# Latent attention on one core: the order of three engines inside a group of two heads

## The chip, the cores and the metric

One core of one Trainium2 chip runs the whole program. The metric is the device time of one execution in microseconds; lower is better. The time of the kernel before is the median of 3 runs.

The engines: PE is TensorE (matmuls; PEld is its weight loads, which run beside them), DVE is VectorE, ACT is ScalarE, POOL is GpSimd, SP issues DMAs. Each engine works through its own list in the order in which it is written, and waits at semaphores for the others.

## What is computed

The reference is two blocks of a network, with float32 throughout. The change touches one operation in the first block, the latent attention (8 heads of 64 + 32 features, 256 context tokens and 1024 latent tokens):

```python
def block_attention(q, k, v, scale):            # per block of 128 queries
    s = jnp.einsum('bhqd,bhkd->bhqk', qi, k) * scale
    p = jax.nn.softmax(s, axis=-1)
    return jnp.einsum('bhqk,bhkd->bhqd', p, v)

# latent queries see context and latent keys, context queries the context keys
a_lat = block_attention(qa_l, concat([ka_c, ka_l]), concat([va_c, va_l]), scale)
a_ctx = block_attention(qa_c, ka_c, va_c, scale)
```

The queries are `rmsnorm(cq) @ w_uq`, whose last 32 features of each head are rotated by position. Everything else in the program (projections, mLSTM, gated linear attention, neighbourhood attention, a second block with an MLP) stands before or behind this loop and stays as it is.

## The kernel before

The attention is a loop over 40 groups in `mla_block`. A group g is a pair of heads and a tile of 128 queries: `groups[g] = (j, t)`. Its two heads are u = 2g (head 0) and u = 2g+1 (head 1). The first 8 groups are of context queries and have 2 key tiles of 128 keys each (short groups); the other 32 are of latent queries and have 10 (long groups).

The scores are made with the keys in the partitions: one key tile gives a 128 x 128 piece of scores, key by query. Head 0 has its scores in three PSUM banks (`S[0]`), head 1 in three others (`S[1]`). A float32 matmul of the source is two matmul instructions in the trace, each with its weight load: a key tile of scores is 2 loads, 10 tiles are 20.

For one head the steps are, in the order in which they depend on each other:

- `score` (TensorE, L1034): the key tiles' scores. A head's first tile waits for the rotated queries (`q_ev`) and until the head before the last in the same banks has been subtracted (`lowered`).
- `tops` (VectorE, L1332): the maximum over the key tiles, for each query and each of the 128 key rows.
- `turn_top` (TensorE, L1043): turns that 128 x 128 piece, so that queries are in the partitions. It waits for `tops`.
- `highest` (VectorE, L1336): one maximum for each query.
- `spread_max` (TensorE, L1047): turns the maxima into a row that stands in all partitions. It waits for `highest`.
- `copy_max` (ScalarE, L1226): copies that row from PSUM.
- `lower` (VectorE, L1342): subtracts the row from all scores. It waits for `copy_max`.
- `soft` (ScalarE, L1237): the exponential.
- `key_sums` (GpSimd, L889 to L894): adds up the key tiles for the softmax's denominator.

Per group come `weigh` (TensorE, L1055: 40 narrow matmuls over both heads' weights and values), `total_up` (L1061: the sums over the partitions), `copy_out` (ScalarE, L1232) and `outputs` (VectorE, L1350 and L1352: reciprocal and product). All of these run one group late: group g-1's stand in the loop body of g.

The queries of group g+2 are made in the body of g: `up_q` (TensorE, L1018, 12 matmuls), `copy_q` (ScalarE, L1222) and `turn_q` (GpSimd, L877, the rotation). `up_q` waits for `copy_out` of the group before, since both use bank `B7`.

The orders are written out by hand. TensorE's body for g is: the first `cut` tiles of head 1's scores, `turn_top` of head 0, the other tiles of head 1, `spread_max` of head 0, `weigh` and `total_up` of g-1, `turn_top` of head 1, three tiles of the next group's head 0 (one in the short groups), `spread_max` of head 1, `up_q`, the other tiles of the next head 0.

VectorE's body is `tops`, `highest` of head 0, `tops` of head 1, `lower` of head 0, `highest` of head 1, `outputs` of g-1, `lower` of head 1. ScalarE's is `copy_max`, `copy_out`, `soft` for head 0, `copy_max` of head 1, `copy_q`, `soft` of head 1.

Of the kernel before, what the change touches and what calls it, by code (L numbers as in the profile page):

```python
# [18 lines left out]
TT = T // P  # L19
# [710 lines left out]
def mla_block(nc, name, U, H, io, v_dram, a_dram, n_dram, f_dram, o_dram, mod, gain, rcol, mod1, ones, ident, eps, ahead, h_late, w_first, banks):  # L730
# [14 lines left out]
    nkt = [TT if t >= 2 else 2 for _, t in groups]  # L745
# [5 lines left out]
    with Stage(nc, name) as s:  # L751
# [154 lines left out]
        def _(pe):  # L906
# [116 lines left out]
            def score(u, tiles):  # L1023
                g, hh = divmod(u, 2)
                j, t = groups[g]
                if tiles[0] == 0:
                    pe.wait_ge(q_ev, 2 * g + 2)
                    if u >= 2:
                        pe.wait_ge(lowered, u - 1)
                    else:  # L1030
                        pe.wait_ge(kv_a, kv_act[len(KV)])
                        pe.wait_ge(kv_d, kv_dve[len(KV)])
                for kt in tiles:
                    last = nc.tensor.matmul(S[hh][:, kt * P:(kt + 1) * P], k[:, j, hh, kt * P:(kt + 1) * P], q[:, g % 3, hh, :],  # L1034
                                            start=True, stop=True)
                if tiles[-1] == nkt[g] - 1:
                    last.then_inc(scored, 1)

            def turn_top(u):
                pe.wait_ge(topped, u + 1)  # L1040
                if u:
                    pe.wait_ge(max_row, u)
                nc.tensor.transpose(TR[:, 0:P], top[:, u % 2, :], ident[:]).then_inc(top_tr, 1)  # L1043

            def spread_max(u):
                pe.wait_ge(maxed, u + 1)
                nc.tensor.transpose(TR[:, P:2 * P], mx[:, u % 2:u % 2 + 1].broadcast_to([P, P]), ident[:]).then_inc(max_mm, 1)  # L1047
# [24 lines left out]
            score(0, range(nkt[0]))  # L1072
            for g in range(NG):
                tiles = range(nkt[g])
                cut = 7 if nkt[g] == TT else 1
                score(2 * g + 1, tiles[:cut])
                turn_top(2 * g)
                score(2 * g + 1, tiles[cut:])
                spread_max(2 * g)
                if g:  # L1080
                    weigh(g - 1)
                    total_up(g - 1)
                turn_top(2 * g + 1)
                if g + 1 < NG:
                    after = range(nkt[g + 1])
                    cut = 3 if nkt[g + 1] == TT else 1
                    score(2 * g + 2, after[:cut])
                    spread_max(2 * g + 1)
                    if g + 2 < NG:
                        up_q(g + 2)  # L1090
                    score(2 * g + 2, after[cut:])
                else:
                    spread_max(2 * g + 1)
            weigh(NG - 1)
# [3 lines left out]
        def _(act):  # L1098
# [125 lines left out]
            def copy_max(u):  # L1224
                act.wait_ge(max_mm, u + 1)
                nc.scalar.activation(low[:, u % 2, :], TR[:, P:2 * P], ACT.Copy).then_inc(max_row, 1)  # L1226
# [7 lines left out]
            def soft(u):  # L1234
                nk = nkt[u // 2] * P
                act.wait_ge(lowered, u + 1)
                nc.scalar.activation(pr[:, u % 4, 0:nk], pr[:, u % 4, 0:nk], ACT.Exp, scale=scale).then_inc(exped, 1)  # L1237
# [3 lines left out]
            for g in range(NG):  # L1241
                copy_max(2 * g)
                if g:
                    copy_out(g - 1)
                soft(2 * g)
                copy_max(2 * g + 1)
                if g + 2 < NG:
                    copy_q(g + 2)
                soft(2 * g + 1)
            copy_out(NG - 1)  # L1250

        @block.vector
        def _(dve):
# [75 lines left out]
            def tops(u):  # L1329
                g, hh = divmod(u, 2)  # L1330
                dve.wait_ge(scored, u + 1)
                nc.vector.reduce_max(top[:, hh, :], S[hh][:, 0:nkt[g] * P].rearrange("p (t q) -> p q t", q=P), AX).then_inc(topped, 1)  # L1332

            def highest(u):
                dve.wait_ge(top_tr, u + 1)
                nc.vector.reduce_max(mx[:, u % 2:u % 2 + 1], TR[:, 0:P], AX).then_inc(maxed, 1)  # L1336

            def lower(u):
                g, hh = divmod(u, 2)
                dve.wait_ge(max_row, u + 1)  # L1340
                shape = [P, nkt[g], P]
                nc.vector.tensor_tensor(pr[:, u % 4, 0:nkt[g] * P].rearrange("p (t q) -> p t q", q=P),  # L1342
                                        S[hh][:, 0:nkt[g] * P].rearrange("p (t q) -> p t q", q=P),
                                        low[:, hh, :].rearrange("p (o q) -> p o q", o=1).broadcast_to(shape), ALU.subtract).then_inc(lowered, 1)
# [28 lines left out]
            for g in range(NG):  # L1373
                tops(2 * g)
                highest(2 * g)
                tops(2 * g + 1)
                lower(2 * g)
                highest(2 * g + 1)
                if g:
                    outputs(g - 1)  # L1380
                lower(2 * g + 1)
# [3674 lines left out]
```

## Time and profile before

| what | value |
|---|---|
| median of 3 runs | 3995.55 us (3993.97 to 3995.95) |
| the profiled execution's own time | 3999.31 us |
| its span | 3997.3 us |
| TensorE busy in the span | 3904.2 us (98%) |
| VectorE / ScalarE / GpSimd busy | 46% / 24% / 23% |
| mean granted TensorE clock | 0.990 |
| the loop's first `up_q` to the next stage's first matmul | 290.74 to 650.49 us |
| one long group in the middle of it | 9.57 us, of which TensorE 9.40, VectorE 7.58, ScalarE 3.65, GpSimd 7.24 busy |

A row of the timeline gives the start and length of an instruction, or of several of a kind in a row (x6), counted from the span's start. What stands in square brackets is how long the engine had been idle before it and whose work ended that. A busy TensorE is a modelled figure: its matmuls overlap, so the starts of its weight loads (PEld) tell more about its pace than the ends of its matmuls.

### The profile page before, as it was taken

The numbers are of one execution on the slowest core, as the hardware profiler recorded it, in microseconds if no ns is written. First come the engines' busy times: TensorE is split into PE (matmuls) and PEld (weight loads), VectorE is DVE, ScalarE is ACT, GpSimd is POOL, SyncE is SP. The second block draws the span as 40 slices with busy tenths as digits, with TensorE's granted clock in tenths as the row PEclk, the third lists the DMA queues.
The fourth block names the chain that finished last, engine by engine and source line by source line (L and its number), as shares of the span: only waits on it lengthen the run. The fifth ranks groups of instructions, "written<-read, shape, count | busy, mean of one in ns | idle before, by whom it ended". The sixth has DMA issues, their size and how long they took to land. (4 is left out here: it accounts for less than half of the span.)

```text
span 3997.3 us, 48524 instructions
## 1 busy us (share of the span) xinstructions
PE 3904.2 (98%) x18394; PEld 2421.4 (61%) x18394; DVE 1856.2 (46%) x3875; ACT 974.9 (24%) x1837; POOL 937.8 (23%) x992
## 2 busy tenths in 40 slices
PE   8999999999999999989999999999999999999998
PEld 4788997776558568567544565656544444444447
DVE  3237775676343366646466322222566452223134
ACT  4223332333124311155324311111123010000000
POOL 0005774001111111133222112122232122222223
PEclk9999999999999999989999999999999999999999
DMA  5420003111211111132131112113243211111113
GB/s 194 157 82 10 9 8 68 42 47 53 85 60 45 51 64 51 56 109 91 53 98 58 48 37 80 42 58 103 96 141 128 79 32 42 46 49 43 42 45 103
DMA packets 113717, 270.25 MB, mean 68 GB/s; under 512 B 15623, under 2 KB 45177, under 8 KB 112398
## 3 DMA queue, kind: packets, MB, share of 16 engines
q1 hardware_dynamic: 106512, 251.81, 19.2%
q0 software_dynamic: 5920, 13.25, 1.3%
q8 instruction: 148, 2.42, 0.3%
q10 hardware_dynamic: 1056, 2.10, 0.1%
q14 instruction: 81, 0.66, 0.1%
HBM read 218.53 MB, written 50.87 MB: 67 GB/s over the span
## 5 line engine op out<-in xcount | busy, mean ns | idle before, releaser
L452 PE MATMUL upper_banks<-sbuf 128*128 128x512 f32 (+1 forms) x2016 | 771.3, 545 | 1.5 <-issue 1.1
L3353 PE MATMUL upper_banks<-sbuf 128*128 128x512 f32 x1400 | 615.6, 595 | 6.9 <-ACT sbuf L3630 3.6
L452 PEld LDWEIGHTS upper_banks<-sbuf 128*128 128x128 f32 x2016 | 382.4, 190 | 388.6 <-issue 373.5
L3353 PEld LDWEIGHTS upper_banks<-sbuf 128*128 128x128 f32 x1400 | 262.6, 191 | 318.8 <-issue 307.5
L2495 PE MATMUL gla_prod<-sbuf 128*128 128x512 f32 x560 | 247.5, 593 | 0.6 <-DVE sbuf L2527 0.6
L608 DVE TENSOR_TENSOR sbuf<-upper_banks,sbuf 128x512 f32<-128x512 f32 (+1 forms) x140 | 81.8, 584 | 283.3 <-PE upper_banks L452 282.7
L404 POOL TENSOR_TENSOR sbuf<-sbuf 128x512 f32<-128x512 f32 x36 | 46.8, 1300 | 655.1 <-DMA sbuf<-in_w_mlp_out 306.4
L1034 PE MATMUL mla_banks<-sbuf 128*128 128x128 f32 x1344 | 172.9, 278 | 6.3 <-DVE sbuf L1342 5.5
L2495 PEld LDWEIGHTS gla_prod<-sbuf 128*128 128x128 f32 x560 | 104.5, 192 | 120.2 <-issue 117.4
L1655 PE MATMUL mls_banks<-sbuf 128*128 128x512 f32 x392 | 175.1, 593 | 0.0
L1034 PEld LDWEIGHTS mla_banks<-sbuf 128*128 128x128 f32 x1344 | 162.0, 194 | 11.7 <-POOL sbuf L877 9.1
L3893 DVE TENSOR_TENSOR sbuf<-upper_banks,sbuf 128x512 f32<-128x512 f32 x75 | 53.5, 715 | 226.3 <-PE upper_banks L3353 222.4
L3558 PE MATMUL upper_banks<-sbuf 128*128 128x512 f32 x336 | 148.6, 604 | 4.8 <-DVE sbuf L4133 2.4
L575 DVE TENSOR_TENSOR sbuf<-upper_banks,sbuf 128x512 f32<-128x512 f32 x48 | 33.1, 690 | 221.3 <-PE upper_banks L452 221.3
L496 ACT ACTIVATE sbuf<-upper_banks 128x512 f32<-128x512 f32 x48 | 28.7, 597 | 429.4 <-PE upper_banks L452 429.4
L1332 DVE TENSOR_REDUCE sbuf<-mla_banks 128x128 f32<-128x1280 f32 (+1 forms) x80 | 102.2, 1278 | 54.0 <-PE mla_banks L1034 54.0
L3558 PEld LDWEIGHTS upper_banks<-sbuf 128*128 128x128 f32 x336 | 64.6, 193 | 88.0 <-issue 81.8
L1655 PEld LDWEIGHTS mls_banks<-sbuf 128*128 128x128 f32 x392 | 71.6, 190 | 75.9 <-issue 74.1
L3384 PE MATMUL upper_banks<-sbuf 128*128 128x256 f32 (+2 forms) x512 | 115.6, 385 | 0.9 <-DVE sbuf L4052 0.6
L891 POOL TENSOR_TENSOR sbuf<-sbuf 128x640 f32<-128x640 f32 x64 | 98.9, 1545 | 59.3 <-ACT sbuf L1237 59.3
L894 POOL TENSOR_TENSOR sbuf<-sbuf 128x128 f32<-128x128 f32 (+1 forms) x192 | 105.2, 548 | 15.1
L3384 PEld LDWEIGHTS upper_banks<-sbuf 128*128 128x128 f32 x512 | 92.9, 225 | 22.4 <-issue 16.7
(565 smaller groups left out, 6665.6 us busy)
## 6 DMA issues: line engine op xcount, KB each, us to landing
sbuf<-in_l_w_in SPq DMA_DIRECT2D x59, 512.0 KB, 4.0
sbuf<-in_w_in SPq DMA_DIRECT2D x52, 512.0 KB, 4.4
sbuf<-in_w_mlp_out SPq DMA_DIRECT2D x40, 512.0 KB, 3.6
sbuf<-in_w_mlp_in SPq DMA_DIRECT2D x32, 512.0 KB, 3.6
sbuf<-in_l_w_mod SPq DMA_DIRECT2D x24, 512.0 KB, 6.3
scratch_gates<-sbuf SPq DMA_DIRECT2D x48, 256.0 KB, 2.0
sbuf<-in_l_w_mod SPq DMA_DIRECT2D x8, 1024.0 KB, 17.0
sbuf<-in_l_w_out SPq DMA_DIRECT2D x16, 512.0 KB, 3.8
```

The source lines that it names most:

```text
L452: last = nc.tensor.matmul(bank_of(n, c)[:, 0:wd], lw[:, k * P:(k + 1) * P], right_operand(c, base, tw, k, o, wd, to), start=k == 0 and c i ...
L608: nc.vector.tensor_tensor(dst, bank_of(n, c)[:, 0:wd], dst, ALU.add).then_inc(dve_done, 1)
L891: nc.gpsimd.tensor_tensor(to, e[:, 0:5 * P], e[:, 5 * P:10 * P], ALU.add).then_inc(partial, 1)
L894: nc.gpsimd.tensor_tensor(to[:, 0:w0], to[:, 0:w0], to[:, o:o + w0], ALU.add).then_inc(partial, 1)
L1034: last = nc.tensor.matmul(S[hh][:, kt * P:(kt + 1) * P], k[:, j, hh, kt * P:(kt + 1) * P], q[:, g % 3, hh, :], start=True, stop=True)
L1332: nc.vector.reduce_max(top[:, hh, :], S[hh][:, 0:nkt[g] * P].rearrange("p (t q) -> p q t", q=P), AX).then_inc(topped, 1)
L1655: last = nc.tensor.matmul(banks[:, n % 2, :], lw[:, kk * P:(kk + 1) * P], right, start=c in ("P1", "P2", "P5") and kk == 0, stop=kk == 3, ...
L2495: last = nc.tensor.matmul(pb, wk, right, start=fresh and kk == 0, stop=kk == 3, skip_group_check=True)
L3353: last = nc.tensor.matmul(pb, lw[:, k * P:(k + 1) * P], rhs, start=k == 0 and c in ("P1", "P2", "P5"), stop=k == 3, skip_group_check=True)
L3384: last = nc.tensor.matmul(dst, lhsT, rhs, start=k == 0, stop=k == KD - 1)
L3558: last = nc.tensor.matmul(banks[:, branch_bank(b, c), :], left[:, o + k * P:o + (k + 1) * P], rhs, start=k == 0 and c in ("P1", "P2", "P5" ...
L3893: nc.vector.tensor_tensor(dst, src, k, ALU.add).then_inc(dve_out, 1)
```

## The change

Three orders change; no instruction is added or taken away.

```diff
             for g in range(NG):
                 tiles = range(nkt[g])
-                cut = 7 if nkt[g] == TT else 1
+                cut = 4 if nkt[g] == TT else 1
                 score(2 * g + 1, tiles[:cut])
                 turn_top(2 * g)
                 score(2 * g + 1, tiles[cut:])
...
                     score(2 * g + 2, after[:cut])
                     spread_max(2 * g + 1)
+                    score(2 * g + 2, after[cut:])
                     if g + 2 < NG:
                         up_q(g + 2)
-                    score(2 * g + 2, after[cut:])
...
                 soft(2 * g)
                 copy_max(2 * g + 1)
+                soft(2 * g + 1)
                 if g + 2 < NG:
                     copy_q(g + 2)
-                soft(2 * g + 1)
...
                 tops(2 * g)
                 highest(2 * g)
+                lower(2 * g)
                 tops(2 * g + 1)
-                lower(2 * g)
                 highest(2 * g + 1)
```

TensorE's list in a long group before, from `turn_top` of head 0 to the next one (a count is in matmuls of the source):

```order
L1043 MATMUL mla_banks<-sbuf 128x128
L1034 MATMUL mla_banks<-sbuf 128x128 x3
L1047 MATMUL mla_banks<-sbuf 128x128
L1055 MATMUL mla_banks<-sbuf 64x128 x20
L1061 MATMUL mla_banks<-sbuf 64x128 x2
L1043 MATMUL mla_banks<-sbuf 128x128
L1034 MATMUL mla_banks<-sbuf 128x128 x3
L1047 MATMUL mla_banks<-sbuf 128x128
L1018 MATMUL mla_banks<-sbuf 128x128 x6
L1034 MATMUL mla_banks<-sbuf 128x128 x14
L1043 MATMUL mla_banks<-sbuf 128x128
```

The 14 tiles in one row are seven of the next group's head 0 and seven of its head 1. The same stretch of the changed kernel:

```order
L1043 MATMUL mla_banks<-sbuf 128x128
L1034 MATMUL mla_banks<-sbuf 128x128 x6
L1047 MATMUL mla_banks<-sbuf 128x128
L1055 MATMUL mla_banks<-sbuf 64x128 x20
L1061 MATMUL mla_banks<-sbuf 64x128 x2
L1043 MATMUL mla_banks<-sbuf 128x128
L1034 MATMUL mla_banks<-sbuf 128x128 x3
L1047 MATMUL mla_banks<-sbuf 128x128
L1034 MATMUL mla_banks<-sbuf 128x128 x7
L1018 MATMUL mla_banks<-sbuf 128x128 x6
L1034 MATMUL mla_banks<-sbuf 128x128 x4
L1043 MATMUL mla_banks<-sbuf 128x128
```

The queries (L1018) have moved behind the seven tiles of the next head 0; of head 1's ten tiles four instead of seven stand ahead of `turn_top`, and six instead of three between it and `spread_max`.

VectorE's list in a long group before, from `tops` of head 0 to `lower` of head 1:

```order
L1332 TENSOR_REDUCE sbuf<-mla_banks 128x128
L1336 TENSOR_REDUCE sbuf<-mla_banks 128x1
L1332 TENSOR_REDUCE sbuf<-mla_banks 128x128
L1342 TENSOR_TENSOR sbuf<-mla_banks,sbuf 128x1280
L1336 TENSOR_REDUCE sbuf<-mla_banks 128x1
L1350 RECIPROCAL sbuf<-sbuf 128x128
L1352 TENSOR_TENSOR sbuf<-sbuf 128x128
L1342 TENSOR_TENSOR sbuf<-mla_banks,sbuf 128x1280
```

And in the changed kernel:

```order
L1332 TENSOR_REDUCE sbuf<-mla_banks 128x128
L1336 TENSOR_REDUCE sbuf<-mla_banks 128x1
L1342 TENSOR_TENSOR sbuf<-mla_banks,sbuf 128x1280
L1332 TENSOR_REDUCE sbuf<-mla_banks 128x128
L1336 TENSOR_REDUCE sbuf<-mla_banks 128x1
L1350 RECIPROCAL sbuf<-sbuf 128x128
L1352 TENSOR_TENSOR sbuf<-sbuf 128x128
L1342 TENSOR_TENSOR sbuf<-mla_banks,sbuf 128x1280
```

Head 0's subtraction (the first L1342) has moved ahead of head 1's maxima (the second L1332).

## Rows read from the trace of the kernel before

**Rows 1.** Windows, long groups: length, busy us (instructions) per engine, granted clock, DMA.

```profile
342.00:640.00 298.00, 291.15 (x3084) 269.18 (x3082) 235.05 (x249) 112.78 (x187) 223.81 (x309) 1.00 0.03 8
```

**Rows 2.** Waits, long groups: who waited for whom: total us, times, longest.

```profile
PEld mla_banks L1043 <- DVE sbuf L1332: 6.3, 30, 0.2
```

**Rows 3.** Timeline, one period: start us, length us, engine, line, operation, count [idle before].

```profile
501.16 0.14 PEld L1043 LDWEIGHTS mla_banks<-sbuf 128*128 128x128 f32 x1 [0.21 <-DVE sbuf L1332]
...
501.53 0.29 DVE L1336 TENSOR_REDUCE sbuf<-mla_banks 128x1 f32<-128x128 f32 x1 [0.42 <-PE mla_banks L1043]
501.89 0.14 PEld L1047 LDWEIGHTS mla_banks<-sbuf 128*128 128x128 f32 x1
...
502.20 1.49 DVE L1332 TENSOR_REDUCE sbuf<-mla_banks 128x128 f32<-128x1280 f32 x1 [0.38 <-PE mla_banks L1034]
...
502.31 0.28 ACT L1226 ACTIVATE sbuf<-mla_banks 128x128 f32<-128x128 f32 x1 [2.47 <-PE mla_banks L1047]
503.61 1.48 DVE L1342 TENSOR_TENSOR sbuf<-mla_banks,sbuf 128x1280 f32<-128x1280 f32 x1
...
504.75 0.14 PEld L1043 LDWEIGHTS mla_banks<-sbuf 128*128 128x128 f32 x1 [0.17 <-issue]
...
505.12 0.29 DVE L1336 TENSOR_REDUCE sbuf<-mla_banks 128x1 f32<-128x128 f32 x1
...
505.20 0.74 PEld L1034 LDWEIGHTS mla_banks<-sbuf 128*128 128x128 f32 x6 [0.31 <-POOL sbuf L877]
...
505.87 0.14 PEld L1047 LDWEIGHTS mla_banks<-sbuf 128*128 128x128 f32 x1
...
505.98 1.42 PEld L1018 LDWEIGHTS mla_banks<-sbuf 128*128 128x128 f32 x12
...
506.62 1.49 DVE L1342 TENSOR_TENSOR sbuf<-mla_banks,sbuf 128x1280 f32<-128x1280 f32 x1
...
507.32 3.21 PEld L1034 LDWEIGHTS mla_banks<-sbuf 128*128 128x128 f32 x28
...
509.19 1.49 DVE L1332 TENSOR_REDUCE sbuf<-mla_banks 128x128 f32<-128x1280 f32 x1 [1.08 <-PE mla_banks L1034]
...
510.74 0.14 PEld L1043 LDWEIGHTS mla_banks<-sbuf 128*128 128x128 f32 x1 [0.21 <-DVE sbuf L1332]
```

**Rows 4.** Timeline, same period and the next: what follows VectorE's second subtraction.

```profile
508.14 1.27 ACT L1237 ACTIVATE sbuf<-sbuf 128x1280 f32<-128x1280 f32 x1
...
509.88 1.54 POOL L891 TENSOR_TENSOR sbuf<-sbuf 128x640 f32<-128x640 f32 x1
...
513.43 0.99 POOL L877 TENSOR_TENSOR sbuf<-sbuf 64x128 f32<-64x128 f32 x2
```

**Rows 5.** Timeline, one period of the short groups.

```profile
304.89 0.14 PEld L1043 LDWEIGHTS mla_banks<-sbuf 128*128 128x128 f32 x1 [0.48 <-DVE sbuf L1332]
...
305.96 0.28 ACT L1226 ACTIVATE sbuf<-mla_banks 128x128 f32<-128x128 f32 x1 [1.09 <-PE mla_banks L1047]
...
306.27 0.42 DVE L1342 TENSOR_TENSOR sbuf<-mla_banks,sbuf 128x256 f32<-128x256 f32 x1 [0.37 <-ACT sbuf L1226]
...
309.77 0.14 PEld L1043 LDWEIGHTS mla_banks<-sbuf 128*128 128x128 f32 x1 [0.48 <-DVE sbuf L1332]
```

**Rows 6.** Timeline, the last two groups.

```profile
625.61 0.14 PEld L1043 LDWEIGHTS mla_banks<-sbuf 128*128 128x128 f32 x1 [0.21 <-DVE sbuf L1332]
...
634.22 0.14 PEld L1043 LDWEIGHTS mla_banks<-sbuf 128*128 128x128 f32 x1
...
638.54 0.29 DVE L1336 TENSOR_REDUCE sbuf<-mla_banks 128x1 f32<-128x128 f32 x1 [0.34 <-PE mla_banks L1043]
...
642.93 4.16 PEld L1055 LDWEIGHTS mla_banks<-sbuf 128*64 128x64 f32 x40 [3.92 <-issue]
```

**Rows 7.** Timeline, the first long group, behind its turn_top of head 1.

```profile
340.82 1.05 PEld L1034 LDWEIGHTS mla_banks<-sbuf 128*128 128x128 f32 x6 [1.32 <-issue]
```

**Rows 8.** Window in the first long group, columns as in rows 1.

```profile
342.00:345.00 3.00, 3.00 (x17) 3.00 (x16) 1.63 (x2) 0.41 (x3) 2.73 (x3) 0.56 0.08 22
```

## The prediction, made before the changed kernel ran

> **What bounds the kernel now.** I read the table of windows first, then the list of waits, then one period of the timeline, since the change touches one loop: the 40 groups of the latent attention, 8 short ones (2 key tiles) and 32 long ones (10 key tiles). In the long groups TensorE is busy 291 of 298 us at full granted clock, VectorE 235, GpSimd 224 [rows 1]. So TensorE bounds it, with little room: what can be won is its idle time, and what can be lost is whatever makes it wait longer.
>
> From here on a group's first head is head 0 (u = 2g), its second head 1 (u = 2g+1). A period runs from one turn_top of head 0 (L1043) to the next: from 501.16 to 510.74, and 13 periods from 501.16 to 625.61 give 9.57 us each [rows 3, 6]. In it TensorE waits in two places that a new order could fill: 0.31 us ahead of the next group's first three score tiles (at 505.20; GpSimd's query rotation is named, but head 0's subtraction, ending at 503.61 + 1.48 = 505.09, releases it just as late), and 0.21 us ahead of turn_top of head 0, for VectorE's maxima [rows 3], the same wait in 30 periods [rows 2]. Together 0.52 us a period. The two waits of 0.17 us called "issue" stay.
>
> What the reader is to see in [rows 3] besides is where VectorE's latencies lie. Between `highest` of head 0 (501.53) and the row that `lower` subtracts, TensorE must turn the maximum (501.89) and ScalarE must copy it (502.31 + 0.28). VectorE doesn't wait for that: it runs `tops` of head 1 in the gap (502.20 to 503.69) and subtracts behind it (503.61). And `tops` of head 1 is over a good microsecond before TensorE asks for it (504.75).
>
> **The change, part by part.** It adds and removes no instruction; it reorders three engines.
>
> *VectorE, head 0's subtraction ahead of head 1's maxima.* The chain that this makes, from TensorE's turn_top of head 0 (time 0), is worked out leg by leg:
> - turn_top to spread_max of head 0 was 0.73 us (501.16 to 501.89) with three score tiles between, six loads. The cut of 4 leaves six tiles between, six loads more; six loads take 0.67 us (505.20 to 505.87) [rows 3]. So 1.40. The maximum itself would be there at about 0.7 (501.53 + 0.29 = 501.82), so the new tiles, not VectorE, hold spread_max back.
> - spread_max's load to ScalarE's copy: 0.42 (501.89 to 502.31) [rows 3]; copy's start to the subtraction, where nothing else stands between: 0.31 (305.96 to 306.27) [rows 5]. The subtraction starts at 2.13.
> - Back to back, two of VectorE's long operations start 1.41 apart (502.20 to 503.61) [rows 3]. `tops` of head 1 starts at 3.54.
> - From `tops` to the turn_top that waits for it: 1.55 (509.19 to 510.74) [rows 3]. turn_top of head 1 loads at 5.09.
> TensorE is ready for it earlier: from spread_max of head 0 to turn_top of head 1 stand the weighing and the sums, 2.86 us (501.89 to 504.75), so 1.40 + 2.86 = 4.26. **TensorE idles 0.83 us there, where it didn't wait for VectorE before.** This is the price of the change: VectorE's two long operations and the two hand-overs, which lay beside each other, now stand in a row.
>
> *The rest of the period on both engines.* VectorE: turn_top of head 1 to `highest` 0.37 (501.16 to 501.53), `highest` to head 1's subtraction 1.50 with the outputs between (505.12 to 506.62) [rows 3], subtraction to the next `tops` 1.41, `tops` to turn_top 1.55: 5.09 + 0.37 + 1.50 + 1.41 + 1.55 = **9.92**. TensorE from turn_top of head 1: 0.14 its own load, 0.67 three tiles, 0.11 spread_max (505.87 to 505.98), seven tiles 1.61 (half of 3.21), the queries 1.34 (505.98 to 507.32), four tiles 0.92 (8 of 28 loads in 3.21) [rows 3]: 5.09 + 4.79 = 9.88. The two loops end within 0.04 us of each other, and the later one counts: 9.92 against 9.57, 0.35 more in each of 29 periods (32 long groups without the first and the last two): **+10.1 us**.
>
> *TensorE, the queries behind the scores.* For themselves they are a gain: `tops` of the next head 0 now runs beside them, 1.34 us earlier, and the 0.31 us wait ahead of the three tiles is gone, because head 0's subtraction ends at 2.13 + 1.48 = 3.61, well before 5.2. But TensorE pays the 0.83 at turn_top of head 1 instead of the 0.52, and VectorE then has no time left over.
>
> *ScalarE, the copy of the queries behind head 1's exponential.* I cost it at nothing. Its cover: the rotated queries are needed by the score tiles one period on, at 5.09 + 0.14 after the next turn_top. Head 1's subtraction starts at 5.09 + 0.37 + 1.50 = 6.96; the exponential follows 1.52 later (506.62 to 508.14), GpSimd's sums 1.74 after that (509.88), and the rotation ends 4.54 after the sums begin (509.88 to 513.43 + 0.99) [rows 3, 4]: 14.76 at the latest, since the row of 509.88 also held back for the sums of head 0. That is 4.84 into the next period of 9.92, and it is asked for at 5.23. The margin is 0.4 us; were it gone, each microsecond late would be one of TensorE's. GpSimd has room otherwise, 224 of 298 us [rows 1]. SP's and GpSimd's queues keep their order.
>
> *Short groups.* `highest` there ends behind the tiles between, so spread_max isn't held back: the subtraction still starts 1.38 after turn_top (304.89 to 306.27) [rows 5]. `tops` follows at +0.34 (0.42 less the 0.07 by which 1.48 exceeds 1.41), turn_top of head 1 at +0.48, `highest` +0.37, subtraction +1.50, `tops` +0.34, turn_top +0.48: 4.89 against 4.88 (304.89 to 309.77). Zero a group; with the step from the last short to the first long group, whose `tops` now hides behind the queries, I take -0.5 for all eight, bounds -1 and +1.
>
> *First long group.* Its weighing is short, so turn_top of head 1 waits longest here; already now TensorE idles 1.32 us ahead of a six-load row that takes 1.05 instead of 0.74, and the granted clock then stands at 0.56 [rows 7, 8], between its two levels of 1.2 and 2.4 GHz. The idle grows, and the slow stretch falls on work that VectorE hides in part. I take 0; -1.3 if the clock stays up, +1.5 if the slow stretch lasts longer.
>
> *The last two groups* make no queries, so nothing hides `tops` and nothing changes on VectorE: the last period but one was 8.61 (625.61 to 634.22) and becomes 9.92, **+1.3**. In the last, `highest` of head 1 stood 4.32 after turn_top (634.22 to 638.54) and comes at 5.09 + 0.37 = 5.46; all from there to the last weighing at 642.93 is unchanged [rows 6]: **+1.1**.
>
> Sum: 10.1 + 1.3 + 1.1 - 0.5 = +12.0 us. The loop ends in a barrier before the next stage, so it passes on whole. The rows come from an execution of 3999.31 us, 3.8 above the median of 3995.55; a difference made from its rows is put on the median: **4007.5 us**.
>
> **The rivals.**
> - *Faster: TensorE's order decides.* If VectorE had 0.83 us to spare at turn_top of head 1, both old waits would be filled: 0.52 x 29 = 15 us less, 3980. For it speaks only that VectorE is busy 235 of 298 us on average [rows 1]; against it that it's a chain with latencies in it, not a sum of busy times. It decides from the point at which the subtraction starts 0.83 earlier, at 1.3, before the six tiles are even through. Chance 6 in 100.
> - *The same.* Two or three legs overlap by more than my rows show and the period lies between 9.57 and 9.75: 0 to 5 us, and the last two groups 2: 3996 to 4003. My legs are read to a hundredth, but the subtraction directly behind a copy was never seen in a long group. 14 in 100.
> - *The clock falls in each period.* An idle of 0.83 us a period could bring the clock down as in the first long group, where 3 us at 0.56 lose 3 x 0.44 = 1.3 us [rows 8]; once a period that is 29 x 1.3 = 38 more, some 4045. Against it: with 0.86 us of idle in four pieces the long groups show 1.00 [rows 1], and the one fall came behind a wait of 1.32 with another close ahead of it. The Trainium skill, in "TensorE: Matmul & The Clock Gate", section "A second HAM failure mode: psum-queue depth-cycling", tells of a kernel whose frequent short idles between groups of matmuls alone made the clock swing between its levels; by that rule this rival would be the forecast, and the rows of the long groups so far don't bear it out. 4 in 100.
> - *It doesn't do what it says*: the order of instructions shows all three moves in every group, so no chance is left for that.
>
> **How the numbers follow.** The forecast has 76 in 100; its own range is set by the period (9.82 to 10.02, a tenth to either side: 7 to 13 us), the short groups (-1 to +1) and the first long one (-1.3 to +1.5): 4003 to 4013. A measurement of this kernel tells 0.2%, 8 us, from no change, so nearly all of it counts as slower. The range reaches down to 3999, half into the case of no change, and up to 4014; it leaves out the faster case, the clock case and the rest. Slower: 76 + 4 = 80; within: 14; faster: 6.
>
> **What would show it right or wrong.** Right: a period of 9.9 us between turn_tops of head 0; a wait of about 0.8 us ahead of turn_top of head 1, ended by VectorE's `tops`; no wait ahead of the next group's three tiles; a subtraction about 2.1 us after turn_top of head 0; VectorE going from head 1's subtraction straight into the next `tops`. Wrong: a period below 9.57; turn_top of head 1 loading before 4.6; a granted clock below 1.00 throughout the long groups; or GpSimd's rotation ending last ahead of the score tiles.

## The result, and the profile after

The changed kernel takes 4026.16 us (median of 4 runs, 4019.90 to 4032.97), the kernel before beside it 3994.76 (4 runs, 3993.89 to 3995.95): a ratio of 1.0077, 95% interval 1.0066 to 1.0089. It is slower by 31.4 us. The forecast of 4007.5 had the sign, and its range ended at 3999 to 4014: about 19 us are missing from it.

The profiled execution of the changed kernel took 4019.9 us, its span is 4018.1. First the rows of busy times of the two pages (share of the span, number of instructions), the kernel before and then the changed one, and then the window over the long groups, with the columns of [rows 1]:

```profile
PE 3904.2 (98%) x18394; PEld 2421.4 (61%) x18394; DVE 1856.2 (46%) x3875; ACT 974.9 (24%) x1837; POOL 937.8 (23%) x992
```

```profile
PE 3897.9 (97%) x18394; PEld 2418.1 (60%) x18394; DVE 1874.8 (47%) x3875; ACT 975.3 (24%) x1837; POOL 937.1 (23%) x992
```

```profile
342.00:640.00 298.00, 268.42 (x2829) 247.04 (x2828) 230.52 (x226) 103.34 (x170) 203.48 (x282) 1.00 0.03 8
```

VectorE is busy 18.6 us more over the whole program (1874.8 against 1856.2 us), with as many instructions (3875) as before. The forty products of `outputs` alone take 34.7 us instead of 11.7. TensorE does less in the same 298 us (268.42 us busy against 291.15), and the granted clock is 1.00, as before: the clock explains nothing in the long groups.

One period, with the columns of [rows 3], from one turn_top of head 0 to the next:

```profile
503.09 0.14 PEld L1043 LDWEIGHTS mla_banks<-sbuf 128*128 128x128 f32 x1 [0.37 <-DVE sbuf L1332]
...
504.49 0.14 PEld L1047 LDWEIGHTS mla_banks<-sbuf 128*128 128x128 f32 x1
...
504.91 0.28 ACT L1226 ACTIVATE sbuf<-mla_banks 128x128 f32<-128x128 f32 x1 [1.69 <-PE mla_banks L1047]
505.22 1.49 DVE L1342 TENSOR_TENSOR sbuf<-mla_banks,sbuf 128x1280 f32<-128x1280 f32 x1 [1.47 <-ACT sbuf L1226]
506.57 0.98 POOL L877 TENSOR_TENSOR sbuf<-sbuf 64x128 f32<-64x128 f32 x2
506.63 1.48 DVE L1332 TENSOR_REDUCE sbuf<-mla_banks 128x128 f32<-128x1280 f32 x1
506.93 0.25 PEld L1061 LDWEIGHTS mla_banks<-sbuf 128*64 128x64 f32 x4
...
508.16 0.14 PEld L1043 LDWEIGHTS mla_banks<-sbuf 128*128 128x128 f32 x1 [0.98 <-DVE sbuf L1332]
...
508.24 0.74 PEld L1034 LDWEIGHTS mla_banks<-sbuf 128*128 128x128 f32 x6
...
508.53 0.29 DVE L1336 TENSOR_REDUCE sbuf<-mla_banks 128x1 f32<-128x128 f32 x1 [0.42 <-PE mla_banks L1043]
508.74 0.94 DVE L1350 RECIPROCAL sbuf<-sbuf 128x128 f32<-128x128 f32 x1
...
509.09 1.54 POOL L891 TENSOR_TENSOR sbuf<-sbuf 128x640 f32<-128x640 f32 x1 [1.54 <-ACT sbuf L1237]
...
509.75 1.02 DVE L1352 TENSOR_TENSOR sbuf<-sbuf 128x128 f32<-128x128 f32 x1
...
510.70 1.48 DVE L1342 TENSOR_TENSOR sbuf<-mla_banks,sbuf 128x1280 f32<-128x1280 f32 x1
...
512.10 1.48 DVE L1332 TENSOR_REDUCE sbuf<-mla_banks 128x128 f32<-128x1280 f32 x1
...
512.29 0.97 PEld L1034 LDWEIGHTS mla_banks<-sbuf 128*128 128x128 f32 x8 [0.30 <-issue]
...
513.63 0.14 PEld L1043 LDWEIGHTS mla_banks<-sbuf 128*128 128x128 f32 x1 [0.37 <-DVE sbuf L1332]
```

The period is 513.63 - 503.09 = 10.54 us, where 9.57 stood [rows 3] and 9.92 was forecast. The reader is to see two things. TensorE waits 0.98 us ahead of turn_top of head 1 (508.16), where it waited 0.17. And the product of `outputs` (L1352, at 509.75) lasts 1.02 us. In the kernel before it lasts 0.29, and starts just ahead of GpSimd's sum (L891) instead of inside it; the first row is `total_up`, which is needed further down:

```profile
504.33 0.25 PEld L1061 LDWEIGHTS mla_banks<-sbuf 128*64 128x64 f32 x4
...
506.35 0.29 DVE L1352 TENSOR_TENSOR sbuf<-sbuf 128x128 f32<-128x128 f32 x1
506.49 1.55 POOL L891 TENSOR_TENSOR sbuf<-sbuf 128x640 f32<-128x640 f32 x1 [1.64 <-ACT sbuf L1237]
```

All 40 products of either kernel, as minimum, median and maximum in nanoseconds, before and then after:

```profile
L1352 DVE TENSOR_TENSOR sbuf<-sbuf x40: 291/293/294, 303.4 to 649.4; 128x128 f32<-128x128 f32 x40
```

```profile
L1352 DVE TENSOR_TENSOR sbuf<-sbuf x40: 292/1022/1026, 302.0 to 678.1; 128x128 f32<-128x128 f32 x40
```

Nothing of this shows as a wait: the instruction has started, and its longer time is counted as busy. 31 of the 40 products last 1.01 to 1.03 us.

The whole loop from the first queries to the next stage grew by 30.6 us: in the profiled execution of after it runs from 288.76 to 679.15, before from 290.74 to 650.49. That is 28.0 us in 29 periods (305.64 us, from 344.97 to 650.61, instead of 277.62), 1.9 in the last period but one (10.53 instead of 8.61), 1.7 behind it, and 1.0 less in the groups ahead. Behind the loop the two kernels are the same; ahead of the loop and behind it the profiled execution of after is 2.0 and 7.9 us shorter, at a slightly higher granted clock (0.992 over the span against 0.990), so that its span is only 20.8 us longer. Its other runs took 4025 to 4033.

### The profile page after: what moved, and what is told of

It is laid out like the page before. It is cut to its first block and busy times, and to the rows that moved or that the text cites. A ratio compares the mean times of both kernels' runs of the same rounds, so it can differ in the third digit from the quotient of the medians.

```text
span 4018.1 us, 48524 instructions
## 1 busy us (share of the span) xinstructions
PE 3897.9 (97%) x18394; PEld 2418.1 (60%) x18394; DVE 1874.8 (47%) x3875; ACT 975.3 (24%) x1837; POOL 937.1 (23%) x992
## 5 line engine op out<-in xcount | busy, mean ns | idle before, releaser
L452 PEld LDWEIGHTS upper_banks<-sbuf 128*128 128x128 f32 x2016 | 382.4, 190 | 388.8 <-issue 374.2
L3353 PEld LDWEIGHTS upper_banks<-sbuf 128*128 128x128 f32 x1400 | 262.0, 190 | 315.8 <-issue 306.1
L1342 DVE TENSOR_TENSOR sbuf<-mla_banks,sbuf 128x1280 f32<-128x1280 f32 (+1 forms) x80 | 101.8, 1272 | 53.4 <-ACT sbuf L1226 53.4
L891 POOL TENSOR_TENSOR sbuf<-sbuf 128x640 f32<-128x640 f32 x64 | 98.5, 1539 | 88.6 <-ACT sbuf L1237 88.6
L3558 PEld LDWEIGHTS upper_banks<-sbuf 128*128 128x128 f32 x336 | 64.2, 192 | 86.5 <-issue 79.7
L1237 ACT ACTIVATE sbuf<-sbuf 128x1280 f32<-128x1280 f32 (+1 forms) x80 | 87.7, 1096 | 90.2 <-DVE sbuf L1342 90.2
```

What stands on the lines that cost most here:

```text
L452: last = nc.tensor.matmul(bank_of(n, c)[:, 0:wd], lw[:, k * P:(k + 1) * P], right_operand(c, base, tw, k, o, wd, to), start=k == 0 and c i ...
L891: nc.gpsimd.tensor_tensor(to, e[:, 0:5 * P], e[:, 5 * P:10 * P], ALU.add).then_inc(partial, 1)
L3353: last = nc.tensor.matmul(pb, lw[:, k * P:(k + 1) * P], rhs, start=k == 0 and c in ("P1", "P2", "P5"), stop=k == 3, skip_group_check=True)
L3558: last = nc.tensor.matmul(banks[:, branch_bank(b, c), :], left[:, o + k * P:o + (k + 1) * P], rhs, start=k == 0 and c in ("P1", "P2", "P5" ...
```

## The experiments

Two explanations were held against each other. *The shared read:* the product has both its inputs in SBUF, and GpSimd's sum L891 (509.09 to 510.63) reads SBUF too; the product, asked for in the midst of the sum, is held until the sum is through. It ends at 509.75 + 1.02 = 510.77, 0.14 us behind the sum's end. *The order:* the serial order itself costs 10.5 us, by legs that were misjudged, and the product only waits for data or lies off the path. All times below are medians, with the kernel before measured on the same chip beside them, and each ratio is to that. Periods are from turn_top of head 0 to the next, in the middle of the long groups.

**e1: the product with one input in SBUF.**

```diff
-  nc.vector.tensor_tensor(stage[:, g % 4, :], raw[:, g % 2, 0:P], stage[:, g % 4, :], ALU.mult)
+  nc.vector.tensor_tensor(stage[:, g % 4, :], S[1][:, 0:P], stage[:, g % 4, :], ALU.mult)
```

> The changed kernel, but the product in outputs (L1352) reads the second head's scores, which lie in PSUM, in place of the raw numerators in SBUF: one SBUF input in place of two, same place, same shape; the attention's outputs are left out of the result. Theory (contention): the product takes 1.02 us in the changed kernel because GpSimd's five-tile sum runs at that time and VectorE's second SBUF input has to wait for it; here it goes back to 0.29 us, the period from 10.54 to the 9.92 that was forecast, and the time to about 4026 - 29 x 0.62 = 4008. Rival (place): the product is long because of where it now stands (a drain, a buffer, the store behind it), whatever it reads: it stays at 1.0, the period at 10.54, the time at 4026.

4007.52 us (7 runs) against 3996.35, ratio 1.003 (1.0019 to 1.0041), period 9.80. All 40 products, and then rows of one period, from its turn_top of head 0 (503.49) and the row ahead of that:

```profile
L1352 DVE TENSOR_TENSOR sbuf<-mla_banks,sbuf x40: 291/292/293, 303.6 to 656.5; 128x128 f32<-128x128 f32 x40
```

```profile
502.50 0.97 PEld L1034 LDWEIGHTS mla_banks<-sbuf 128*128 128x128 f32 x8
...
503.49 0.14 PEld L1043 LDWEIGHTS mla_banks<-sbuf 128*128 128x128 f32 x1
...
508.56 0.14 PEld L1043 LDWEIGHTS mla_banks<-sbuf 128*128 128x128 f32 x1 [0.98 <-DVE sbuf L1332]
...
508.93 0.29 DVE L1336 TENSOR_REDUCE sbuf<-mla_banks 128x1 f32<-128x128 f32 x1 [0.42 <-PE mla_banks L1043]
...
509.49 1.54 POOL L891 TENSOR_TENSOR sbuf<-sbuf 128x640 f32<-128x640 f32 x1 [1.54 <-ACT sbuf L1237]
...
510.15 0.29 DVE L1352 TENSOR_TENSOR sbuf<-mla_banks,sbuf 128x128 f32<-128x128 f32 x1
510.36 1.48 DVE L1342 TENSOR_TENSOR sbuf<-mla_banks,sbuf 128x1280 f32<-128x1280 f32 x1
```

The product starts 0.66 us into GpSimd's sum, as in the changed kernel, and lasts 0.29. Nothing has changed but the place of one input, and of the 31.4 us over the kernel before 11.2 are left; in the traces the loop is 7.4 us longer than before instead of 30.6. What is left looks like the forecast: a wait of 0.98 us ahead of turn_top of head 1, none ahead of the other two rows of TensorE, and a period 0.12 below the 9.92. That the time meets the forecast of 4007.5 is luck: the ratio's interval reaches from 7.6 to 16.4 us over the kernel before, and the loop grew by 7.4, not by the 12.0 of the sum.

**e2: the product on GpSimd.** Here nothing is left out: GpSimd multiplies behind the sums of head 0, VectorE only makes the reciprocal.

```diff
-  nc.vector.reciprocal(stage[:, g % 4, :], raw[:, g % 2, P:2 * P])
-  dve.drain()
-  nc.vector.tensor_tensor(stage[:, g % 4, :], raw[:, g % 2, 0:P], stage[:, g % 4, :], ALU.mult).then_inc(oev, 1)
+  nc.vector.reciprocal(stage[:, g % 4, :], raw[:, g % 2, P:2 * P]).then_inc(o_rec, 1)
...
+            def product(g):
+                pool.wait_ge(o_rec, g + 1)
+                nc.gpsimd.tensor_tensor(stage[:, g % 4, :], raw[:, g % 2, 0:P], stage[:, g % 4, :], ALU.mult).then_inc(oev, 1)
...
                 key_sums(2 * g)
+                if g:
+                    product(g - 1)
                 key_sums(2 * g + 1)
...
```

> The changed kernel with the product of outputs moved from VectorE to GpSimd, behind head 0's sums, so that VectorE and GpSimd can't meet there. Theory (contention): VectorE goes from highest of head 1 to head 1's subtraction in 1.2 to 1.4 us in place of 2.17; VectorE's chain ends at 9.7 and TensorE's own loop at 9.88, so the period is about 9.9 and the time about 4007. Rival (place): GpSimd's product takes a microsecond too, or the subtraction is held by something else; period 10.2 or more, 4017 or more.

4005.55 us (8 runs) against 3996.35, ratio 1.0025 (1.0014 to 1.0035), period 9.76. GpSimd needs 0.46 us for each product, and the period shows that it has them to spare. All 40 of them, then the rows of VectorE's subtraction of head 1 beside the five-tile sum, in the same kernel:

```profile
L901 POOL TENSOR_TENSOR sbuf<-sbuf x40: 452/457/460, 306.1 to 657.7; 128x128 f32<-128x128 f32 x40
```

```profile
501.69 1.55 POOL L891 TENSOR_TENSOR sbuf<-sbuf 128x640 f32<-128x640 f32 x1 [1.45 <-ACT sbuf L1244]
...
502.22 1.49 DVE L1349 TENSOR_TENSOR sbuf<-mla_banks,sbuf 128x1280 f32<-128x1280 f32 x1
```

The subtraction reads PSUM and SBUF and keeps its 1.49 us although it starts inside the sum: together with e1, it's the second input in SBUF that matters, not GpSimd's company.

**e9: GpSimd's sum in two halves.** The same contention, with less to wait for.

```diff
-  nc.gpsimd.tensor_tensor(to, e[:, 0:5 * P], e[:, 5 * P:10 * P], ALU.add).then_inc(partial, 1)
+  m = 5 * P // 2
+  nc.gpsimd.tensor_tensor(to[:, 0:m], e[:, 0:m], e[:, 5 * P:5 * P + m], ALU.add)
+  nc.gpsimd.tensor_tensor(to[:, m:5 * P], e[:, m:5 * P], e[:, 5 * P + m:10 * P], ALU.add).then_inc(partial, 1)
```

> The changed kernel with GpSimd's five-tile sum (1.54 us) issued as two halves of 320 columns, some 0.86 us each by the durations of its rows (640 columns 1.54, 128 columns 0.45). The product of outputs starts 0.66 after the sum, inside the first half. If VectorE gets its turn between two GpSimd instructions, the product ends about 0.1 after the first half: 0.35 to 0.45 us in place of 1.02, the period 9.9 to 10.0 in place of 10.54, the time some 16 to 18 less than the changed kernel in the same call. If GpSimd's next instruction comes first, the product waits for the second half as well: 1.1 to 1.2 us, a period of 10.6 to 10.8, 3 to 8 us more than the changed kernel.

4005.45 us (8 runs) against 3995.28, ratio 1.0025 (1.0014 to 1.0036), period 9.86. Line numbers are higher by two from here on in this kernel:

```profile
511.85 0.86 POOL L892 TENSOR_TENSOR sbuf<-sbuf 128x320 f32<-128x320 f32 x1 [1.40 <-ACT sbuf L1239]
...
512.52 0.34 DVE L1354 TENSOR_TENSOR sbuf<-sbuf 128x128 f32<-128x128 f32 x1
512.67 0.91 POOL L893 TENSOR_TENSOR sbuf<-sbuf 128x320 f32<-128x320 f32 x1
```

The product comes 0.67 us into the first half and ends at 512.86, 0.15 behind that half's end (512.71). It doesn't wait for the whole sum, but for the one instruction that was running.

**e10: the changed kernel again, unaltered, on the chip of e9.**

> The changed kernel itself, unaltered, beside the run above on the same chip: period 10.54, product 1.02, 4020 to 4033 as in its first runs. It shows how far runs of one kernel differ in the stages behind the attention, where the granted clock falls at different places.

4023.43 us (4 runs), ratio 1.0073 (1.0058 to 1.0088), period 10.53. The result stands, and e9's gain of 18 us isn't the chip's. In the traces e9's loop is 11.4 us longer than before, the changed kernel's again 30.7.

**e5: the kernel before, with the product made twice.** The first of two puts its result where the denominators have been read for the last time; the second is the real one.

```diff
+  nc.vector.tensor_tensor(raw[:, g % 2, P:2 * P], raw[:, g % 2, 0:P], stage[:, g % 4, :], ALU.mult)
   nc.vector.tensor_tensor(stage[:, g % 4, :], raw[:, g % 2, 0:P], stage[:, g % 4, :], ALU.mult).then_inc(oev, 1)
```

> The kernel before with the product of outputs issued twice (first into the spent denominators, then as before). The first starts 0.14 us ahead of GpSimd's five-tile sum as now, the second falls into it. Theory (contention): first 0.29 us, second about 1.5 us (506.57 to the sum's end at 508.04 and a little), so head 1's subtraction starts at 508.1 in place of 506.62; the next head 1's scores wait for its end at 509.6 in place of starting at 508.9, and the period becomes about 10.1 in place of 9.57: 4010. Rival (the product is long only where the change puts it): both 0.29, hidden in VectorE's idle of 1.08 us ahead of tops; period 9.57 and 3996.

4013.35 us (4 runs) against 3994.69, ratio 1.0046 (1.0031 to 1.0061), period 10.15. The second product's 40 rows (the first stays at 0.29), then one period:

```profile
L1353 DVE TENSOR_TENSOR sbuf<-sbuf x40: 283/1630/1634, 303.6 to 668.4; 128x128 f32<-128x128 f32 x40
```

```profile
505.43 0.29 DVE L1352 TENSOR_TENSOR sbuf<-sbuf 128x128 f32<-128x128 f32 x1
...
505.58 1.54 POOL L891 TENSOR_TENSOR sbuf<-sbuf 128x640 f32<-128x640 f32 x1 [1.14 <-ACT sbuf L1237]
505.64 1.63 DVE L1353 TENSOR_TENSOR sbuf<-sbuf 128x128 f32<-128x128 f32 x1
```

Two like instructions stand side by side: the first, started 0.15 us ahead of the sum, lasts 0.29; the second, started 0.06 us behind it, lasts 1.63 and ends at 507.27, again 0.15 behind the sum's end (507.12). Head 1's subtraction comes behind it, and TensorE then waits 0.54 us for the next head 1's banks. So the kernel before escaped by 0.14 us, and the order of the change isn't needed to lose to the sum.

**e4: VectorE's move alone**, in the kernel before.

```diff
+                lower(2 * g)
                 tops(2 * g + 1)
-                lower(2 * g)
```

> The kernel before with only head 0's subtraction ahead of head 1's maxima on VectorE; TensorE's order (cut of 7, queries ahead of the scores) and ScalarE's stay. By the legs turn_top of head 1 waits 0.8 us as in the changed kernel. By the theory of contention the product falls into GpSimd's sum as well, since head 0's exponential comes earlier against outputs: about 0.9 us long, head 1's subtraction at 7.06 after turn_top of head 0, the next head 1's scores wait for its end, period 10.2, 29 x 0.63 + 2 = +20: 4015. Rival (place, or the queries' move, makes the product long): product 0.29, subtraction at 6.3, period 10.1 from the maxima of head 0 alone.

4020.07 us (4 runs) against 3996.35, ratio 1.0064 (1.0049 to 1.0079), period 10.14. The product's 40 rows, and one period from turn_top of head 1 on:

```profile
L1352 DVE TENSOR_TENSOR sbuf<-sbuf x40: 292/1021/1028, 302.6 to 668.5; 128x128 f32<-128x128 f32 x40
```

```profile
504.98 0.14 PEld L1043 LDWEIGHTS mla_banks<-sbuf 128*128 128x128 f32 x1 [0.98 <-DVE sbuf L1332]
...
505.91 1.54 POOL L891 TENSOR_TENSOR sbuf<-sbuf 128x640 f32<-128x640 f32 x1 [1.13 <-ACT sbuf L1237]
...
506.57 1.02 DVE L1352 TENSOR_TENSOR sbuf<-sbuf 128x128 f32<-128x128 f32 x1
...
509.11 1.64 PEld L1034 LDWEIGHTS mla_banks<-sbuf 128*128 128x128 f32 x14 [0.30 <-issue]
```

This one move brings both the wait of 0.98 us and the long product. What follows is TensorE's wait at 509.11: the next head 1's seven tiles, 14 loads, want the banks from which head 1's late subtraction still reads (it starts behind the product, at 507.52, and lasts 1.48). A short group takes 5.31 us here, 0.42 more than before.

**e3: the queries' move alone**, on TensorE and ScalarE, VectorE and the cut as before.

```diff
                     spread_max(2 * g + 1)
+                    score(2 * g + 2, after[cut:])
                     if g + 2 < NG:
                         up_q(g + 2)
-                    score(2 * g + 2, after[cut:])
...
                 copy_max(2 * g + 1)
+                soft(2 * g + 1)
                 if g + 2 < NG:
                     copy_q(g + 2)
-                soft(2 * g + 1)
```

> The kernel before with only the queries behind the next head's scores (TensorE) and the copy of the queries behind the exponential (ScalarE); VectorE's order and the cut of 7 stay. By the forecast's own legs VectorE's maxima of head 0 are then ready before TensorE wants to turn them: the wait of 0.21 ahead of turn_top goes, the wait of 0.31 ahead of the three tiles stays, the product stays ahead of GpSimd's sum (0.29 us): period 9.28, 29 x 0.29 = 8 us and about 1 more in the first long group: 3986. Rival: the late queries are part of the loss (copy or rotation ends last): period 9.57 or more, 3995 or more.

3983.23 us (6 runs) against 3996.35, ratio 0.9968 (0.9955 to 0.998): **faster by 13 us than the kernel before**, period 9.33.

```profile
511.41 0.14 PEld L1043 LDWEIGHTS mla_banks<-sbuf 128*128 128x128 f32 x1
...
515.51 0.74 PEld L1034 LDWEIGHTS mla_banks<-sbuf 128*128 128x128 f32 x6 [0.31 <-POOL sbuf L877]
...
516.65 0.29 DVE L1352 TENSOR_TENSOR sbuf<-sbuf 128x128 f32<-128x128 f32 x1
516.79 1.55 POOL L891 TENSOR_TENSOR sbuf<-sbuf 128x640 f32<-128x640 f32 x1 [1.40 <-ACT sbuf L1237]
...
520.75 0.14 PEld L1043 LDWEIGHTS mla_banks<-sbuf 128*128 128x128 f32 x1
```

The wait of 0.21 us ahead of turn_top of head 0 is gone (511.41 and 520.75 have none), since `tops` of head 0 runs beside the queries; the 0.31 ahead of the three tiles stays (515.51). The product keeps its lead of 0.14 us over the sum. 0.24 in 29 periods is 7.0 us; a short group takes 4.38 instead of 4.89, which for seven is 3.6 more. Another 1.9 come from the first long group (9.33 instead of 11.21), and they are hardly the order's: TensorE has the same idles there as before, 0.91 and 1.32 us, but in this execution the granted clock stays at 1.00 behind them, where it fell to 0.56 [rows 8]. Why, no run shows.

**e8: the same with eight tiles ahead of turn_top** instead of seven, to win the wait at 515.51 by an earlier maximum.

```diff
-                cut = 7 if nkt[g] == TT else 1
+                cut = 8 if nkt[g] == TT else 1
```

> The queries behind the scores as in the run of that move alone (VectorE's order of before), with a cut of 8. Head 1's scores end 0.22 earlier against turn_top, so tops and subtraction of head 0 too, and the wait ahead of the three tiles falls from 0.31 to about 0.1; spread_max then waits about 0.2 for the maximum. Period 9.26 to 9.33 against 9.33: 0 to 2 us less, 3981 to 3984.

3987.56 us (10 runs) against 3994.69, ratio 0.9979 (0.997 to 0.9989), periods of 9.33 to 9.35 and 9.39 to 9.42 in turn. Faster than before, and no better than e3. The trace shows where the gain goes: the tile that now stands ahead of turn_top of head 0 adds its 0.22 us there, but spread_max still loads 0.77 us behind turn_top (0.78 in e3), with two tiles between instead of three, since it waits for the maximum. What comes back is 0.06 us ahead of the weighing and 0.08 to 0.14 ahead of the three tiles (a wait of 0.23 and 0.17 in turn instead of 0.31), together no more than the tile costs.

**e6: the cut of four alone**, in the kernel before.

```diff
-                cut = 7 if nkt[g] == TT else 1
+                cut = 4 if nkt[g] == TT else 1
```

> The kernel before with only the cut of 4 in place of 7 (TensorE: six tiles in place of three between turn_top and spread_max of head 0). By the legs: head 1's scores end 0.67 later, so tops and subtraction of head 0 (which stand behind them) end 0.67 later and the three tiles of the next head 0 wait for that; period 9.57 + 0.67 = 10.2, 29 x 0.67 = 19 us and some more at the ends: 4016. Rival: the wait at turn_top of head 0 takes it up (fewer tiles ahead of it), period within 0.1 of 9.57, 3996.

4012.08 us (4 runs) against 3994.69, ratio 1.004 (1.0025 to 1.0055), period 10.24.

```profile
509.63 0.14 PEld L1043 LDWEIGHTS mla_banks<-sbuf 128*128 128x128 f32 x1 [0.88 <-DVE sbuf L1332]
```

With three tiles fewer to hide `tops`, TensorE waits 0.88 us ahead of turn_top of head 0 instead of 0.21: 0.67 more, the whole growth of the period. The size was expected, the place not: the wait ahead of the next head 0's three tiles hardly changes (0.32 us), and it's the wait at turn_top, which the rival named, that grows. The product lasts 0.29.

**e7: the changed kernel with the old cut of seven.**

```diff
-                cut = 4 if nkt[g] == TT else 1
+                cut = 7 if nkt[g] == TT else 1
```

> The changed kernel with the cut of 7 in place of 4. By the legs the subtraction of head 0 comes 0.67 earlier and turn_top of head 1 still waits (0.98 in the changed kernel). With the product held by GpSimd's sum as in the run of VectorE's order alone, head 1's subtraction ends at 8.6 after turn_top of head 0 and the seven tiles behind it (1.6) make the period 10.14, the same as there: 29 x 0.40 = 12 less than the changed kernel, 4014. If the product's wait were only a matter of TensorE's later spread_max, the period would fall to 9.8 and the time to about 4006.

4016.90 us (4 runs) against 3994.69, ratio 1.005 (1.0035 to 1.0065), period 10.14.

```profile
502.12 0.14 PEld L1043 LDWEIGHTS mla_banks<-sbuf 128*128 128x128 f32 x1
...
506.57 0.14 PEld L1043 LDWEIGHTS mla_banks<-sbuf 128*128 128x128 f32 x1 [0.98 <-DVE sbuf L1332]
...
508.16 1.03 DVE L1352 TENSOR_TENSOR sbuf<-sbuf 128x128 f32<-128x128 f32 x1
```

The cut of four only costs the change, 0.40 us a period (10.54 against 10.14): with seven tiles ahead, turn_top of head 1 comes 4.45 us after that of head 0 instead of 5.07 and waits the same 0.98, since spread_max, and with it `lower` and `tops`, comes earlier by what TensorE has less to do. The product is as long as in the changed kernel, at 0.66 us into the sum.

## Why the prediction missed

*VectorE's chain from turn_top of head 0 to turn_top of head 1: right.* Leg by leg the changed kernel's timeline shows 1.40 to spread_max, 0.42 to the copy, 0.31 to the subtraction (2.13 after turn_top, as forecast), 1.41 to `tops`, 1.53 to turn_top of head 1: 5.07 where 5.09 was forecast. The wait there is 0.98, of which 0.17 is the pause that stood there before: 0.81, forecast 0.83. The serial order does what the prediction says it does, and it was the only part that named a loss.

*The rest of VectorE's loop: here it failed.* The step is "`highest` to head 1's subtraction 1.50 (505.12 to 506.62)". It measured 510.70 - 508.53 = 2.17, 0.67 more, and 0.62 of it is in the period (10.54 against 9.92; the other legs were 0.05 shorter). 29 times 0.62 is 18.0, and the last two groups grew by 1.3 more than forecast for the same reason; with the 12.0 of the sum and 0.5 less in the groups ahead that is 30.8, against 30.6 in the loop and 31.4 in the medians. The leg was read from a period in which the outputs between the two were not what held the subtraction back: there it waited for the copy, and the product was through at 506.64 and had started 0.14 us ahead of GpSimd's sum. In the new order the product keeps its distance from turn_top of head 1: 1.60 us before (504.75 to 506.35), 1.59 after (508.16 to 509.75). GpSimd's sum hangs on something else: through ScalarE's `copy_out` and exponential it follows `total_up`, 2.16 us behind it in either kernel (504.33 to 506.49, 506.93 to 509.09). `total_up` doesn't wait for VectorE, turn_top of head 1 now does, 0.81 us longer than before. So the very wait that the prediction had found takes the product from 0.14 us ahead of the sum to 0.66 behind its start. In e4, where only VectorE's order is changed, the sum starts 0.93 us after turn_top of head 1 as in the changed kernel (505.91, 504.98); in e3, with VectorE's order as before, 1.73. The leg without the contention is 1.43 (e1: 510.36, `highest` at 508.93), so the term was even a little too large, by 0.07: with the other legs it's the 0.12 by which e1's period is below 9.92. That makes 3.2 us in 29 periods; with 0.9 in the last two groups and 0.5 in the groups ahead, by e1's trace, the sum of 12.0 was 4.6 too high for a loop without the contention. The contention itself therefore costs more than the 19 us that are missing, 23 by the loops of after and e1. That it does, and not another part of the order, is shown from three sides: one input elsewhere (e1), the product elsewhere (e2), a shorter sum (e9) each give 4005 to 4008; and e5 makes a like loss, 19 us, in the old order.

The Trainium skill says it in "SBUF — State Buffer", section "Who interferes with whom": a VectorE instruction with two SBUF inputs contends with a GpSimd instruction that reads SBUF, and whoever issues second is blocked until the first is done. The trace agrees for VectorE, with 0.29 us when ahead, 1.02 and 1.63 when behind, and 0.29 with one input in PSUM. It doesn't show GpSimd blocked: in the kernel before the sum starts 0.15 us ahead of the product's end and lasts 1.54 to 1.56, where sums without a product beside them take 1.53 to 1.54. And no run sets the product beside a GpSimd instruction that only writes SBUF. The prediction costed the outputs as one leg and never asked what GpSimd runs beside them.

*No wait ahead of the three tiles: right* (508.24 has none). *The next head 1's four tiles: missed.* They wait 0.30 us (512.29), because they want the banks that the late subtraction of head 1 reads until 512.18. It is a consequence of the long product: in e1 the row (502.50) isn't preceded by a wait. The same holds for the 0.37 us ahead of turn_top of head 0, 0.21 before and none in e1 (503.49).

*ScalarE's copy of the queries: right, at nothing.* GpSimd's rotation ends at 506.57 + 0.98 = 507.55, and the tiles that need it load at 508.24, 0.7 us later; 0.4 was forecast.

*Short groups, first long group, last groups.* In the same stretches as in [rows 5 to 8] a short group takes 4.80 us, 0.09 less; the step to the first long group 6.83, 0.62 less; the first long group 11.14 (it was 11.21). Together it's 1.0 less where 0.5 less was forecast. The last period but one grew by 1.92 where 1.3 was forecast: the product's 0.62. The end of the last group:

```profile
661.14 0.14 PEld L1043 LDWEIGHTS mla_banks<-sbuf 128*128 128x128 f32 x1 [0.37 <-DVE sbuf L1332]
...
666.58 0.29 DVE L1336 TENSOR_REDUCE sbuf<-mla_banks 128x1 f32<-128x128 f32 x1 [0.42 <-PE mla_banks L1043]
...
671.64 4.17 PEld L1055 LDWEIGHTS mla_banks<-sbuf 128*64 128x64 f32 x40 [4.58 <-issue]
```

`highest` of head 1 comes 5.44 after turn_top of head 0 (forecast 5.46), and from there to the last weighing it's 5.06 instead of 4.39 [rows 6], again the 0.67 of the long product.

*The rivals.* The clock held at 1.00 with 0.37, 0.98 and 0.30 us of idle in each period (503.09, 508.16, 512.29), so the rival with a falling clock fell, and the rule of the Trainium skill cited with it isn't borne out by this kernel. The prediction's argument that the one fall of the clock came behind a wait of 1.32 us with another close ahead is weaker than it looked, as in e3 the same waits bring no fall. The faster case fell with its condition: VectorE had nothing to spare. But its gain was there to be had without VectorE's move: e3 fills one of the two old waits and wins 13 us, 7 of them in the periods. The prediction had said that the queries behind the scores "for themselves" are a gain, and gave no time for them alone.

*The parts of the change.* Against the kernel before: the queries' move alone -13 us, VectorE's alone +24, the cut alone +17, all together +31. That the three add up to 28, within the noise of 31, doesn't make them independent. In a period of the long groups the queries' move wins 0.24 us alone and nothing beside VectorE's (10.14 in e4 and in e7), and the cut costs 0.67 alone and 0.40 beside the two others. The kernel with the lowest time is e3, 0.32% faster than the kernel before, and by the two ratios (0.9968 and 1.0077) about 1.1% faster than the changed one.

## What to carry to other kernels

Before an order of VectorE's or GpSimd's instructions is changed, list those VectorE instructions that take two inputs from SBUF, and look at what GpSimd runs at their new place: a lead of 0.14 us over a long sum may be all that keeps them short. A leg taken over from the old order is only good for the new one if the same thing ends last in it; otherwise split it into its instructions. Ask also what a new wait shifts: it moves everything behind it against the engines that don't wait. And test the parts of a change one by one, since here the part that wins alone, the queries' move, wins next to nothing once VectorE's is in.

## What the runs showed of the hardware

- A VectorE product of 128 x 128 with both inputs in SBUF, 0.29 us alone, lasts 1.02 us when it starts 0.66 us into a GpSimd sum of 1.54 us, and 1.63 us when it starts 0.06 us into it; it ends 0.14 to 0.15 us after the sum. Started 0.14 us ahead, it isn't touched. With one input in PSUM it takes 0.29 us at 0.66 us into the same sum (e1, all 40 products at 0.29). GpSimd's sum takes 1.53 to 1.56 us in all these cases but one (1.65, in e5's first long group).
- The time appears as busy, not as a wait: the forty products' busy time rose from 11.7 to 34.7 us with the number of instructions the same. The duration of a single instruction, against the same line before, tells of it.
- The block is by the single GpSimd instruction: with the sum cut in two, VectorE's product gets in between the halves (0.34 us).
